# Writing an expert item's weighted rows by token, and scattering them as whole rows

## The reference

```python
def moe(xt, w_router, b_router, w_gate, b_gate, w_up, b_up, w_down, b_down):
    logits = (xt @ w_router + b_router).astype(jnp.float32)
    top_val, top_idx = lax.top_k(logits, TOP_K)            # 4 of 32 experts
    top_w = jax.nn.softmax(top_val, axis=-1)
    ...                                                    # rows sorted by expert, in blocks of 128
    def expert_block(args):
        xblk, e = args
        gate = jnp.minimum(xblk @ w_gate[e] + b_gate[e], SWIGLU_LIMIT)
        up = jnp.clip(xblk @ w_up[e] + b_up[e], -SWIGLU_LIMIT, SWIGLU_LIMIT)
        h = (up + 1.0) * gate * jax.nn.sigmoid(SWIGLU_ALPHA * gate)
        return h @ w_down[e] + b_down[e]
    yb = lax.map(expert_block, (xb, block_e)).reshape(P, D)
    y = jax.ops.segment_sum(yb.astype(jnp.float32) * row_w[:, None], row_tok, num_segments=T + 1)[:T]
```

## Time and profile before

| | us |
|---|---|
| median of three runs | 2564.54 |
| lowest and highest | 2564.26, 2574.02 |
| the profiled execution, its own time | 2564.66 |
| its span in the profile | 2562.8 |

### The profile page before, as it was taken

How to read it: one execution, slowest core, us unless ns; L and a number is a source line. 1 busy time by engine, 2 the same in 40 slices (tenths; PEclk the granted TensorE clock), 3 DMA queues, 4 the chain that set the end, 5 groups by cost and what they waited for, 6 DMA issues and landing times.

```text
span 2562.8 us, 54558 instructions
## 1 busy us (share of the span) xinstructions
PE 2263.5 (88%) x21771; PEld 1083.6 (42%) x21772; DVE 857.8 (33%) x1261; ACT 531.3 (21%) x1209; POOL 642.9 (25%) x631
## 2 busy tenths in 40 slices
PE   5999999998987699999989979799889898999960
PEld 3575756775552234443433433233333333334320
DVE  4155465363452222321322323123212323132213
ACT  5122213222442111111211111111111111111111
POOL 5000000000133132323233333333333323232342
PEclk9999999999986899999999989899999899999985
DMA  8112110135034677596899897899777797999954
GB/s 270 33 33 74 34 58 17 58 110 214 33 140 133 234 277 283 164 340 224 307 390 373 304 364 261 314 327 338 249 246 268 272 381 244 347 373 365 397 176 143
DMA packets 227008, 587.48 MB, mean 229 GB/s; under 512 B 26506, under 2 KB 98306, under 8 KB 226786
## 3 DMA queue, kind: packets, MB, share of 16 engines
q1 hardware_dynamic: 133794, 338.47, 35.0%
q10 hardware_dynamic: 55504, 197.22, 19.6%
q0 software_dynamic: 37648, 50.92, 9.7%
HBM read 548.73 MB, written 37.78 MB: 229 GB/s over the span
## 4 chain that ended last, share of the span: by engine, by line
PE 41%; DMA 39%; issue 9%; DVE 6%; POOLq 2%; ACT 2%; POOL 1%; ACTq 0%; DVEq 0%; SPq 0%
DMA y_rows<-yrow,idx_s 31%; PE ps L1673 10%; DMA xg<-xn_rows,idx_g 7%; PE ps L1459 5%; PE ps L1703 5%; PE ps L1455 4%; PE ps L1560 4%; PE ps L1465 2%; PE ps L1516 2%; PE ps L1462 2%; DVE xr L1339 2%; POOLq L426 1%; PE ps L1611 1%; PE ps L1538 1%; PE ps L1431 1%
## 5 line engine op out<-in xcount | busy, mean ns | idle before, releaser
L1673 PE MATMUL ps<-w_gu_e,xT 128*32 128x512 f32 x9216 | 1013.7, 599 | 58.0 <-DMA w_gu_e<-in_w_up_dram 31.2
L1703 PE MATMUL ps<-w_down_e,hT 128*32 128x256 f32 x9216 | 529.8, 391 | 111.9 <-issue 75.7
L1673 PEld LDWEIGHTS ps<-w_gu_e,xT 128*32 128x32 f32 x9216 | 300.6, 111 | 745.7 <-issue 698.6
L658 POOL DMA_INDIRECT y_rows<-yrow,idx_s x188 | 324.8, 1728 | 642.0 <-DMA y_rows<-yrow,idx_s 581.0
L1703 PEld LDWEIGHTS ps<-w_down_e,hT 128*32 128x32 f32 x9216 | 305.2, 113 | 350.9 <-issue 169.1
L1316 DVE STREAM_TRANSPOSE gu_t<-ps 128x1024 f32<-128x1024 f32 x94 | 111.9, 1228 | 498.2 <-PE ps L1673 497.4
L907 ACT ACTIVATE xT<-xr,fm 128x128 f32<-128x128 f32 x384 | 153.0, 481 | 515.3 <-PE ps L1673 508.2
L923 ACT ACTIVATE yrow<-ps,slot_tab 128x256 f32<-128x256 f32 x188 | 73.8, 475 | 810.6 <-DMA y_rows<-yrow,idx_s 724.6
L1339 DVE STREAM_TRANSPOSE xr<-xg 128x1024 f32<-128x1024 f32 x49 | 60.9, 1244 | 527.9 <-DMA xg<-xn_rows,idx_g 527.9
L645 POOL DMA_INDIRECT xg<-xn_rows,idx_g x196 | 219.9, 1122 | 61.7 <-issue 58.5
L609 POOL DMA_INDIRECT slot_rows<-slot_row,slot_at x32 | 31.3, 980 | 686.9 <-DVE slot_row L1226 679.2
(11 more groups left out here) (275 smaller groups left out, 1469.8 us busy)
## 6 DMA issues: line engine op xcount, KB each, us to landing
w_down_e<-in_w_down_dram ACTq DMA_DIRECT2D x368, 512.0 KB
w_gu_e<-in_w_gate_dram SPq DMA_DIRECT2D x256, 512.0 KB
w_gu_e<-in_w_up_dram SPq DMA_DIRECT2D x256, 512.0 KB
w_ring<-in_w_ada_dram SPq DMA_DIRECT2D x17, 1024.0 KB, 5.2
w_ring<-in_w_in_dram SPq DMA_DIRECT2D x20, 512.0 KB, 5.2
w_first<-in_w_ada_dram SPq DMA_DIRECT2D x7, 1024.0 KB, 12.4
x_all<-in_x_dram SPq DMA_DIRECT2D x2, 2048.0 KB, 10.5
w_out<-in_w_out_dram SPq DMA_DIRECT2D x8, 512.0 KB, 8.5
```

What stands on the lines that cost most here:

```text
L658: G.indirect_dma_start(y_quarters, bass.IndirectOffsetOnAxis(ap=idx_s[:, g:g + 1].bitcast(U32), axis=0), yrow[:, g, :], None, compute_op=A ...
L1673: last = T.matmul(ps[j * GROUP:(j + 1) * GROUP, g, :].rearrange("p (w b f) -> p w b f", w=2, f=GROUP), xT[:, k, g * GROUP:(g + 1) * GROUP] ...
L1703: last = T.matmul(ps[j * GROUP:(j + 1) * GROUP, 4 + g // 2, g % 2 * QUARTER:(g % 2 + 1) * QUARTER], hT[:, g, k, :], w_dn[:, k, j * QUARTER ...
```

## The change

ScalarE no longer writes `yrow` with one instruction of 128x256 for a group, but with four of 32x256: quarter j of group g goes from partitions 32j to 32j + 31 of `ps` to partitions 32g to 32g + 31 of `yrow`, columns 256j to 256j + 255. So `yrow` holds one token a partition, all 1024 columns. One scatter of 128 rows of 4 KB then adds an item onto `y_rows`. Its indices are a column of a new table `row_tab`, which VectorE makes once ahead of the loop with four instructions from `slot_tab`; POOL copies the column to `idx_s`. The scatter of item i stands behind all four gathers of item i + 4. The spare rows for unused slots grow from 32 to 128.

```diff
@@ slots (VectorE, place)
-                V.tensor_scalar(lo_j[:, t, :], pos_j[:, t, :], GROUP - 1, None, ALU.bitwise_and)
+                V.tensor_scalar(lo_j[:, t, :], pos_j[:, t, :], BLOCK - 1, None, ALU.bitwise_and)
@@ POOL, ahead of the loop
-            pool.dma_start(y_dram[SEQ:SEQ + GROUP, :], box[0][0:GROUP, 0:D]).then_inc(y_added, 16)
+            pool.dma_start(y_dram[SEQ:SEQ + BLOCK, :], box[0][:, 0:D]).then_inc(y_added, 16)
@@ POOL
-            def scatter_begun(m):
-                pool.wait_ge(yr_ready, m + 1)
-                apart(pool)
-                slots_of(m, idx_s, sidx_made)
-            def scatter(m, g):
-                pool.wait_ge(y_added, m * (16 * GROUPS) + 16 * (Y_ZERO + g))
-                apart(pool)
-                G.indirect_dma_start(y_quarters, bass.IndirectOffsetOnAxis(ap=idx_s[:, g:g + 1].bitcast(U32), axis=0),
-                                     yrow[:, g, :], None, compute_op=ALU.add).then_inc(y_added, 16)
+            def scatter(m):
+                col = item_column(pool, m)
+                pool.wait_ge(y_added, m * 16 + 16 * Y_ZERO)
+                apart(pool)
+                G.tensor_copy(idx_s[:], row_tab[:, bass.ds(col >> 2, 1)]).then_inc(sidx_made, 1)
+                pool.wait_ge(sidx_made, m + 1)
+                pool.wait_ge(yr_ready, m + 1)
+                apart(pool)
+                G.indirect_dma_start(y_dram, bass.IndirectOffsetOnAxis(ap=idx_s[:].bitcast(U32), axis=0), yrow[:],
+                                     None, compute_op=ALU.add).then_inc(y_added, 16)
             with pool.Fori(0, n_before) as i:
                 gather_begun(i + 4)
-                scatter_begun(i)
                 for g in range(GROUPS):
-                    scatter(i, g)
                     gather(g)
-            for m in (n_before, n_last):
-                scatter_begun(m)
-                for g in range(GROUPS):
-                    scatter(m, g)
+                scatter(i)
+            scatter(n_before)
+            scatter(n_last)
@@ ScalarE, weighted_rows
-                act.wait_ge(y_added, m * (16 * GROUPS) + 16 * Y_ZERO)
+                act.wait_ge(y_added, m * 16 + 16 * Y_ZERO)
                 apart(act)
                 for g in range(GROUPS):
-                    last = A.activation(yrow[:, g, :], ps[:, 4 + g // 2, g % 2 * QUARTER:(g % 2 + 1) * QUARTER],
-                                        ACT.Copy, scale=slot_tab[:, bass.ds(col + g, 1), 1:2].bitcast(F32).rearrange(
-                                            "p o s -> p (o s)"))
+                    for j in range(4):
+                        js = slice(j * GROUP, (j + 1) * GROUP)
+                        last = A.activation(yrow[g * GROUP:(g + 1) * GROUP, j * QUARTER:(j + 1) * QUARTER],
+                                            ps[js, 4 + g // 2, g % 2 * QUARTER:(g % 2 + 1) * QUARTER], ACT.Copy,
+                                            scale=slot_tab[js, bass.ds(col + g, 1), 1:2].bitcast(F32).rearrange(
+                                                "p o s -> p (o s)"))
@@ VectorE, ahead of the loop, behind rows_turned(1)
+            dve.wait_ge(slots_in, 16 * 4)
+            for g in range(GROUPS):
+                gs = slice(g * GROUP, (g + 1) * GROUP)
+                last = V.tensor_scalar(row_tab[gs, :], slot_tab[gs, g:NCOL:GROUPS, 0], 0.25, spare[gs, 0:1], ALU.mult,
+                                       ALU.add)
+            last.then_inc(row_tab_made, 1)
```

More of the change, by code:

```diff
@@ L129, in hybrid_block_kernel @@
         slot_tab = region(64, 72)("slot_tab", NCOL, 2, dt=I32)
+        row_tab = region(169.5, 170.5)("row_tab", NCOL // GROUPS, dt=I32)
         r = region(104, 108)
@@ L160, in hybrid_block_kernel @@
         r = region(149, 157)
-        hT, yrow = r("hT", GROUPS, KT, GROUP), r("yrow", GROUPS, QUARTER)
+        hT, yrow = r("hT", GROUPS, KT, GROUP), r("yrow", D)
         sig_t = region(161, 165)("sig_t", GROUPS, KT, GROUP)
```

31 lines of the change are left out of this document (16 added, 15 removed).

## The result

Measured: 2508.69 us (median of 4 runs, 2506.66 to 2512.47) against 2566.33 for the kernel before (4 runs): ratio 0.9772, 95% interval 0.9746 to 0.9797. The gain is 57.6 us where I had forecast 109, and the time lies 9 us above my range. The profiled execution took 2506.66 us, with a span of 2504.8.

What follows compares the result with a forecast made beforehand. Bound: TensorE idle behind a cycle of four scatters in a row and hand-overs, 36.4 us an item. Savings 39.4 + 31 + 33.5 + 6 - 1 = 109 us took 2564.7 to 2456 us, range 2420 to 2500.

Steps and rivals of the forecast that it cites:

- Rival E: The one scatter lands later than four did, 2.9 us more in each of 27 items: 2633 us, chance 0.05.
- The five waits of items 27 to 36: Waits ahead of down steps: 28.9 us and 10.5 us of slower steps all go, 39.4 us.
- The small experts: Down-step waits at items 19 and 20, 22, 25, 44, partly kept by weight loads: 31 us saved, between 12 and 58.
- rival B: Weights don't bind in items 19 to 44, all 57 us of waits and slow steps there go: 2424 us, chance 0.12.
- Waits for weights that there were: TensorE's existing 31.2 us of waits in stretches of full DMA: 6 us saved, between 0 and 12.
- ScalarE's term: ScalarE's 16 pieces take 6.0 us an item, 4.4 more, hidden beside gate_up in the loop; bounds 1.6 and 7.6.
- The scatter's term: One scatter of 128 rows of 4 KB lands in 10 us, estimated 8.4 to 10.9, against a quarter's median 7.4.
- rival D: POOL's queue cuts 4 KB rows into four packets each, issue 4 x 1.6 us, landing about 14: 2468 us, chance 0.08.
- The end: From the last down steps to the read of the sum, done at 2493: 33.5 us saved, between 28 and 36.
- A: The forecast itself: no down step waits for a scatter any more, 2456 us, chance 0.64.
- C: Weights take more: TensorE runs into loads at the five waits too, half of these come back: 2500 us, chance 0.08.
- F: Nothing moves: landing near 29 us, or the scatter falls behind gathers that land late: 2560 us, chance 0.03.

Runs made afterwards that it cites:

- e9: The changed kernel word for word, run again on chip 11: 2472.78 us, ratio 0.9618 to the kernel before.
- e15: The kernel of e14 with each w_down loaded in four transfers of two slices in place of eight: 2467.11 us on chip 10.
- e1: The kernel before with only ScalarE's writes cut into 16 pieces of 32x256, four quarter scatters kept: 2709.31 us.
- e8: The changed kernel with the scatter's index made ahead of the gathers and half of every later w_down load left out: 2442.60 us.
- e12: The kernel before with POOL's four gathers of an item ahead of its four scatters, not between them: 2525.96 us, ratio 0.9825.
- e2: The changed kernel with ScalarE writing four 128x256 blocks in place of 16 pieces, without regrouping by token (sums not right): 2455.56 us.
- e14: The changed kernel with ScalarE writing only the groups an item has, yrow zeroed once at the start: 2477.90 us on chip 10.

## Why the prediction was wrong, step by step

The first measurement and e9 differ by 35.9 us by their medians (33.6 in the spans) with one text, and e9 differs from the kernel before by 91.6 in the spans (2562.8 to 2471.2), where 109 were forecast. So the miss has two parts: a change of TensorE's pace, which the sum held at nothing, and 17 us in the terms. On chip 11 the changed kernel lies within the range.

**The pace (34 to 36 us): the failed step.** The prediction costed every TensorE step at its duration before, 14.00 us for a down step of four groups and 10.4 a group, as if only waits could change, and gave no reason why these should stay. From the start of item 2's gate/up to that of item 45's down step the first measurement took 1546.0 us and e9 1511.4 (from the matmuls' starts). Nearly all of these 34.6 us arise behind POOL's copy of `idx_s`: matmul by matmul, the lag of the first run on e9 grows by 33 us within the first 2 us behind the 45 copies in this stretch. That is where the loss lies; e15 keeps this copy and doesn't have the loss, so the copy alone is not its cause. Timeline of the changed kernel there (start, us, engine), first measurement:

```profile
1207.31 0.27 PEld L1678 LDWEIGHTS ps<-w_gu_e,xT 128*32 128x32 f32 x4 [0.16 <-issue]
1207.74 0.14 PEld L1678 LDWEIGHTS ps<-w_gu_e,xT 128*32 128x32 f32 x2 [0.16 <-issue]
1207.80 0.19 POOL L652 COPY idx_s<-row_tab 128x1 int32 x1
1208.76 0.16 PEld L1678 LDWEIGHTS ps<-w_gu_e,xT 128*32 128x32 f32 x3 [0.88 <-issue]
1208.83 1.64 POOL L656 DMA_INDIRECT y_rows<-yrow,idx_s  x1 [0.84 <-POOL idx_s L652]
1209.50 0.17 PEld L1678 LDWEIGHTS ps<-w_gu_e,xT 128*32 128x32 f32 x5 [0.58 <-issue]
1210.26 0.27 PEld L1678 LDWEIGHTS ps<-w_gu_e,xT 128*32 128x32 f32 x7 [0.59 <-issue]
1210.69 0.27 PEld L1678 LDWEIGHTS ps<-w_gu_e,xT 128*32 128x32 f32 x4 [0.16 <-issue]
```

and e9 in the same place:

```profile
1207.71 0.14 PEld L1678 LDWEIGHTS ps<-w_gu_e,xT 128*32 128x32 f32 x4 [0.29 <-issue]
1208.14 0.14 PEld L1678 LDWEIGHTS ps<-w_gu_e,xT 128*32 128x32 f32 x4 [0.29 <-issue]
1208.57 0.14 PEld L1678 LDWEIGHTS ps<-w_gu_e,xT 128*32 128x32 f32 x4 [0.29 <-issue]
```

In e9 four loads come every 0.43 us, close together (0.14 us). In the first measurement they are spread over 0.27 us, at the same 0.43 most of the time, and from 1207.74 to 1210.26 ten loads take 2.5 us, for which 1.1 would do.

**What bounded the kernel before: right in the main.** e1 shows the chain's price. (The turn at 1522.04 writes the rows of item 18, not 19, as item 19's down step starts behind it. So there are 28 items to 2505.77 and the mean cycle is 35.1 us, not 36.4; the turns mostly come 29 to 33 and 38 to 43 us apart by turns, so this mean is not the chain's own length. Rival E uses these numbers, the sum doesn't.) The five waits of items 27 to 36 were costed at 39.4 us; between the starts of gate/up 27 and 38, e9 gains 41.0 on the kernel before.

**The small experts: right in kind, too high.** Items 19 and 20 gave 11.7 us (14.4), item 22 3.3 (6), item 25 6.0 (10.7), and item 44 not 0 but a loss of 9.6: the down step starts 5.4 us earlier and gate/up of item 46 then waits 8.5 us for its weights. Sum 11.4 for 31. That the weights bind there is right (e8); but of the 57.7 us of waits and slow steps there, which rival B has in full, these items keep a fifth, where the forecast kept half.

**Waits for weights that there were: too low.** I took 6 us. Items 13 to 18 gave 9.9 and items 38 to 41 8.9, most of it such waits. At 13 to 18 no down step before them had been late, so the loads didn't start earlier: more bytes moved in the same time (349 GB/s from 1235 to 1480 us in e9, 333 before). e12, with the four scatters kept, has 2.5 of these 9.9 us, so most of it seems to go with the four scatters; how was not tested. The errors of the last two paragraphs cancel: to the start of down step 45, 75.4 us were forecast and 70.4 came. That a good sum came from two bad terms is not to the method's credit.

**The order of POOL's work: not costed.** The prediction gives the whole loop to four scatters becoming one. e12 shows that the gathers out of the chain alone give 24 to 67 us on chip 11. The row for it was there: the gather behind the fourth scatter, used at 1523.23.

**ScalarE's term: 6.0 us forecast, 7.65 measured,** at the upper bound. The four 128x256 writes overlap, each further one 0.366 us; the sixteen small ones don't: 7.65 / 16 = 0.478 each for 0.466 of duration. The spacing of the large ones was carried over to another form. The estimate by the Trainium skill (ScalarE: Activation LUTs, What ACT_TABLE_LOAD costs), 0.40 a piece and 6.4 us, is low too, and its rule that partitions don't count holds (0.466 us for 32 of them, 0.475 for 128). The overlap failed as well: the prediction hides ScalarE's turn beside `gate_up`, but for 1 us at the items of one group. Between gate/up of item 2 and the down step of item 45 e2, with the short turn, takes 1504.4 us and e9 1511.4, so it cost 7.0 us there and 6.3 at the end. Behind the one-group items 12, 34 and 37, TensorE waits 2.7, 3.3 and 2.6 us ahead of down steps 11, 33 and 36, where e2 has under 0.9 each. This is the second:

```profile
1954.75 15.94 PE L1708 MATMUL ps<-w_down_e,hT 128*32 128x256 f32 x256 [3.27 <-ACT yrow L921]
```

A down step that still waits for ScalarE inside the loop was among the prediction's own signs of being wrong. ScalarE's turn starts 4.2 us behind the end of down step 32, since its queue first issues eight transfers, lasts 7.65 us, and ends 2.6 us behind the end of the short gate/up step.

**The scatter's term: 10 us forecast, 6.5 measured,** below the lower bound of 8.4. One packet a row held (17536 packets of POOL's queue against 37648), so rival D is out. The growth with the bytes was sized about right: the fastest landing rose from 3.6 to 6.1 us, where 1.0 to 3.5 were to be added. What failed is the base. The 7.4 us are the median of quarters in the old chain, and half of the whole scatters land within 0.4 us of the fastest one. Why the quarters took so much over their own fastest was not tested.

**The end: 33.5 us forecast, 22 came** (61.3 to 39.5 from the end of down step 45 to the read of the sum). e9, against the earlier trace rows:

```profile
2389.88 6.25 PE L1708 MATMUL ps<-w_down_e,hT 128*32 128x256 f32 x112 [1.31 <-issue]
2393.57 4.33 ACTq L940 DMA_DIRECT2D w_down_e<-in_w_down_dram  x8
2398.84 7.64 ACT L921 ACTIVATE yrow<-ps,slot_tab 32x256 f32<-32x256 f32 x16 [4.42 <-issue]
2407.33 13.17 PE L1708 MATMUL ps<-w_down_e,hT 128*32 128x256 f32 x192 [11.20 <-ACT yrow L921]
...
2420.86 7.64 ACT L921 ACTIVATE yrow<-ps,slot_tab 32x256 f32<-32x256 f32 x16 [14.38 <-PE ps L1708]
...
2429.27 1.57 POOL L656 DMA_INDIRECT y_rows<-yrow,idx_s  x1 [15.18 <-ACT yrow L921]
...
2435.65 4.00 SPq L521 DMA_DIRECT2D y_all<-y_rows  x8
```

The forecast had the last down step end 15.5 us behind the one before; it was 24.4. ScalarE's queue first issues eight transfers, which I had set beside down's work, so its turn begins 2.7 us late; it lasts 1.65 longer; and the step itself takes 13.17. But e2, with a turn of 1.57 us, ends that step 24.2 us behind the one before as well:

```profile
2397.51 5.46 PE L1706 MATMUL ps<-w_down_e,hT 128*32 128x256 f32 x56 [5.19 <-issue]
2406.20 10.29 PE L1706 MATMUL ps<-w_down_e,hT 128*32 128x256 f32 x136 [3.23 <-DMA w_down_e<-in_w_down_dram]
```

Its last slice arrives 13.9 us behind down step 45's end; I had said 13.5. What failed at the end is the next count, "there at 2479, the last down step ends at 2481": a step of three groups wants the last slice in its first pass, and 136 of its 192 matmuls come after, 7.4 us at full pace and 10.3 here. In e14, whose last down step has no wait within it, it ends 21.2 us behind the one before. For item 22 the prediction counts this rightly. The remaining 2.8 us are ScalarE's last turn with its hand-over (8.0 for 6.5) and the last scatter (7.15 from ScalarE's end to the read, for 5.8).

**Chances.** A, the mechanism forecast, is what happened in the main; B, C, D, E and F did not. The range was too narrow because it held the durations of TensorE's own steps as given.

## What to carry to other kernels

When several edits that have nothing in common all "fix" the same loss, run the unedited program again before explaining any of them; a first measurement of one load on one chip is one sample. In a sum of removed waits, ask of each step that waits for weights in which pass the last slice is wanted, and what stands in the issuing engine's queue ahead of its turn. And split a change that moves two things (here the order of gathers and the count of scatters) before giving one of them the whole gain.

## What the runs showed of the hardware that I had not expected

- One program text runs at two paces of TensorE, at the same granted clock: weight loads of 1094 us and 4398 matmuls in 360 us on chip 11, 1306 to 1367 us and 4317 to 4353 elsewhere; 2472.8 us against 2494.6 to 2508.7. The kernel before doesn't have it on chip 15 (4404). Nor has the changed kernel with four w_down transfers in place of eight (4394 on chip 10, 4388 on chip 15), though its weight loads stay spread out there (1298 and 1326 us). Cause open.
- ScalarE's 32x256 pieces out of PSUM come at 0.478 us each, whether or not they move to other partitions, where 128x256 writes come at 0.366. VectorE takes 0.482 for the same piece.
- An adding scatter of 128 rows of 4 KB lands 6.5 us after its issue in the median and 6.1 at least; one of 1 KB rows took 7.4 in the median of the old chain and 3.6 at least.
